# Six expert slots instead of four, with the residual parked in DRAM, in a hybrid attention, delta-rule and MoE layer

## The reference

```python
x = x + g1 * mix
h = rms_norm(x, norm2_w) * (1.0 + sc2) + sh2
x = x + g2 * hier_moe(h, ...)
...
def hier_moe(h, ...):               # 32 experts in 4 groups of 8
    grp = jnp.argmax(grp_logits, axis=-1)
    ...
    top_p, top_i = lax.top_k(jax.nn.softmax(in_grp, axis=-1), TOP_K)     # 2 of the group's 8
    wts = p_grp * top_p / jnp.sum(top_p, axis=-1, keepdims=True)
    ...
    hid = silu(h @ w_exp_gate[e]) * (h @ w_exp_up[e])       # 1024 -> 256, twice
    hid = hid * combine[..., None]
    return einsum('blef,efd->bld', hid, w_exp_down)         # 256 -> 1024
```

## Time and profile before

| what | us |
|---|---|
| median of three runs | 1172.69 |
| profiled execution, its own time | 1173.27 |
| its span in the profile | 1171.5 |
| PE busy in the span | 1029.5 (88%) |
| VectorE busy | 433.0 (37%) |
| ScalarE busy | 311.7 (27%) |
| POOL busy | 164.0 (14%) |
| weights of the 28 experts loaded after the routing | 88.1 MB |

### The profile page before, as it was taken

One profiled execution on the slowest core, in us unless ns is written; L12 is line 12 of the kernel. 1 busy time (PEld: TensorE's weight loads), 2 busy tenths in 40 slices (PEclk: granted clock), 3 DMA queues, 4 the chain that ended last, 5 costly groups with the idle time before them and its releaser, 6 DMA issues.

```text
span 1171.5 us, 14600 instructions
## 1 busy us (share of the span) xinstructions
PE 1029.5 (88%) x5595; PEld 562.0 (48%) x5595; DVE 433.0 (37%) x845; ACT 311.7 (27%) x619; POOL 164.0 (14%) x257
## 2 busy tenths in 40 slices
PE   4999999999998889989999999999919997797870
PEld 2444456666554679988544444444513332232220
DVE  1433036787775864645501200224460111100116
ACT  4122144566652434324310000111211111111111
POOL 0100020011000327770300000000110121101110
PEclk9999999999999999999999999999959999988995
DMA  9821152436110111300371110142535999999956
GB/s 387 346 90 46 70 183 88 190 116 216 73 72 16 42 39 41 98 8 1 109 284 72 72 72 10 63 166 85 216 103 192 396 401 422 422 424 423 423 226 269
DMA packets 43644, 204.20 MB, mean 174 GB/s; under 512 B 16736, under 2 KB 22320, under 8 KB 31536
## 3 DMA queue, kind: packets, MB, share of 16 engines
q1 hardware_dynamic: 32576, 171.92, 37.3%
q0 software_dynamic: 10416, 30.45, 7.3%
q10 hardware_dynamic: 576, 0.82, 0.2%
HBM read 191.79 MB, written 19.76 MB: 181 GB/s over the span
## 4 chain that ended last, share of the span: by engine, by line
PE 75%; DVE 11%; issue 5%; DMA 5%; ACT 2%; POOL 2%; SPq 0%; POOLq 0%; DVEq 0%; ACTq 0%
PE bank L1717 25%; PE bank L2311 11%; PE bank L1839 7%; PE bank L2332 5%; PE bank L2156 3%; PE bank L2154 3%; PE bank L1681 2%; PE bank L1998 2%; PE bank L1888 2%; DMA arena<-in_w_up 2%; PE bank L2299 1%; PE bank L2008 1%; PE bank L1732 1%; DMA arena<-in_w_blocks 1%; PE bank L1824 1%
## 5 line engine op out<-in xcount | busy, mean ns | idle before, releaser
L1717 PE MATMUL bank<-arena 128*128 128x512 f32 x672 | 292.6, 591 | 0.0
L1717 PEld LDWEIGHTS bank<-arena 128*128 128x128 f32 x672 | 125.4, 189 | 151.8 <-issue 151.8
L2311 PE MATMUL bank<-arena 128*32 128x512 f32 x1152 | 140.5, 642 | 32.1 <-issue 30.8
L1839 PE MATMUL bank<-arena 128*128 128x320 f32 x384 | 120.0, 454 | 0.0
L2311 PEld LDWEIGHTS bank<-arena 128*32 128x32 f32 x1152 | 42.4, 117 | 117.9 <-issue 117.9
L1839 PEld LDWEIGHTS bank<-arena 128*128 128x128 f32 x384 | 69.7, 192 | 35.7 <-issue 11.2
L1649 DVE TENSOR_TENSOR arena<-arena,bank 128x256 f32<-128x256 f32 x18 | 7.6, 421 | 174.6 <-ACT arena L1104 174.6
L1493 DVE TENSOR_TENSOR arena<-arena,bank 128x512 f32<-128x512 f32 x10 | 6.9, 688 | 168.1 <-PE bank L2156 168.1
L2332 PE MATMUL bank<-arena 128*32 128x512 f32 x576 | 65.8, 595 | 1.0 <-DVE arena L1642 1.0
L1026 ACT ACTIVATE arena<-bank 128x512 f32<-128x512 f32 x20 | 12.0, 598 | 145.7 <-PE bank L1717 145.7
L1104 ACT ACTIVATE arena<-bank 128x256 f32<-128x256 f32 x18 | 6.9, 385 | 164.2 <-PE bank L2311 164.2
(11 more groups left out here) (315 smaller groups left out, 1387.7 us busy)
## 6 DMA issues: line engine op xcount, KB each, us to landing
arena<-in_w_up SPq DMA_DIRECT2D x32, 2048.0 KB, 18.1
arena<-in_w_blocks SPq DMA_DIRECT2D x27, 2048.0 KB, 8.0
arena<-in_w_down SPq DMA_DIRECT2D x32, 1024.0 KB, 21.9
arena<-y_scratch SPq DMA_DIRECT2D x10, 512.0 KB, 7.3
arena<-in_bias POOLq DMA_DIRECT2D x3, 1536.0 KB, 10.7
arena<-mod_scratch POOLq DMA_DIRECT2D x8, 512.0 KB, 10.9
arena<-in_x SPq DMA_DIRECT2D x5, 512.0 KB, 7.0
gram_scratch<-arena SPq DMA_DIRECT2D x10, 256.0 KB, 2.5
```

What stands on the lines that cost most here:

```text
L1717: last = mm(bank, hT[:, k, tok0[i]:tok0[i] + P], w[:, k, :], start=(k == 0), stop=(k == KC - 1))
L1839: last = mm(banks[5 + half][:, 0:HTOK], w[:, k, :], hT[:, k, half * HTOK:(half + 1) * HTOK], start=(k == 0), stop=(k == KC - 1))
L2311: last = mm(banks[2 + e % 2][at, :], rowsT[e % 2][:, k, at], eup[expert % SLOTS_W][:, k, :], start=(k == 0), stop=(k == KC - 1))
```

## The change

The four slots become six, numbered 0 to 5; experts 0 to 5 are loaded before the routing. Experts 6 to 23 use slot e % 6, experts 24 to 31 slot e % 4. The list of rows keeps its 2304 places and 18 tiles: ten experts of 96 rows, twenty of 64, and two of 32. The last tile thus holds experts 29, 30 and 31.

The room for slot 4's up is taken from `gate2_bc` and the small tensors behind it, that for slot 5's up from the residual `x2` itself; the down weights of both stand in pieces (two of 0.5 MB, four of 0.25 MB) in places that are free then. So `x2` is written to DRAM (`x_scratch`) after the mixing part, and `gate2_bc` is no longer loaded early; both are loaded by SP (`residual_back`) behind the last expert load, and VectorE waits for them before its last steps. The router gets one operation more for the offsets and two for the capacities. The norm's unused square goes to a part of `merged`, and some semaphores are merged under one name.

```diff
-SLOTS_W = 4
-N_WIDE, WIDE, NARROW = 8, 96, 64
+SLOTS_W, DENSE_W = 6, 4
+N_BIG, N_SMALL = 4, 2
+WIDE, NARROW, SMALL = 96, 64, 32
 N_RANKED = N_EXPERTS - SLOTS_W
-SLOTS = N_WIDE * WIDE + (N_EXPERTS - N_WIDE) * NARROW
+ROWS_OF = [WIDE] * (SLOTS_W + N_BIG) + [NARROW] * (N_RANKED - N_BIG - N_SMALL) + [SMALL] * N_SMALL
+SLOTS = sum(ROWS_OF)
+SLOT_OF = [e % SLOTS_W if e < N_EXPERTS - 2 * DENSE_W else e % DENSE_W for e in range(N_EXPERTS)]
...
+        def before(e):
+
+            return max(q for q in range(e) if SLOT_OF[q] == SLOT_OF[e])
...
+            def residual_back():
+                for c in range(2):
+                    row = bass.AP(t["mod_scratch"].tensor, 3 * KC * 2 * P + c * P, [[0, P], [2 * P, KC], [1, P]])
+                    sp.dma_start(gate2_bc[:, c, :].rearrange("p (k n) -> p k n", k=KC), row).then_inc(S["y_out"], 16)
+                for i in range(T):
+                    sp.dma_start(x2[:, i, :], t["x_scratch"][i]).then_inc(S["y_out"], 16)
...
             sp.wait_ge(S["x2_ready"], NHALF * T)
+            for i in range(T):
+                sp.dma_start(t["x_scratch"][i], x2[:, i, :]).then_inc(S["y_out"], 16)
             up_in(3)
+            sp.wait_ge(S["logit_mm"], 3)
+            down_in(5)
+            sp.wait_ge(S["y_out"], 16 * T)
+            sp.wait_ge(S["h_ready"], 2 * T)
+            sp.wait_ge(S["ssq_ready"], T + 1)
+            up_in(5)
+            down_in(4)
...
                 for n in range(TILES):
                     for q in range(SLOTS_W, N_EXPERTS):
-                        if last_tile(q - SLOTS_W) == n:
+                        if last_tile(before(q)) == n:
                             sp.wait_ge(S["eup_mm"], n + 1)
                             ranked_up(q)
...
+                sp.wait_ge(S["down_mm"], max(last_tile(e) for e in range(N_EXPERTS) if SLOT_OF[e] >= DENSE_W) + 1)
+                residual_back()
...
-            step(v.tensor_scalar(lists[:, L_CAP + SLOTS_W:L_CAP + N_EXPERTS], rank, float(n_big), float(NARROW - WIDE), ALU.is_lt, ALU.mult))
+            ranked_cap = lists[:, L_CAP + SLOTS_W:L_CAP + N_EXPERTS]
+            step(v.tensor_scalar(ranked_cap, rank, float(N_BIG), None, ALU.is_lt))
+            step(v.scalar_tensor_tensor(ranked_cap, rank, float(N_RANKED - N_SMALL), ranked_cap, ALU.is_lt, ALU.add))
+            step(v.tensor_scalar(ranked_cap, ranked_cap, -1.0, float(NARROW - WIDE), ALU.add, ALU.mult))
```

More of the change, by code:

```diff
@@ L259, in build @@
         gate1_bc = cut(2, D)
+        gate2_at = top[0]
         gate2_bc = cut(2, D)
@@ L322, in build @@
         rows_out = [flat(hT)[:, (2 + n) * D:(3 + n) * D] for n in range(3)]
-        slot_f = flat(merged)[:, 4 * D:4 * D + 2 * TILES]
-        empty = flat(merged)[:, 4 * D + 2 * TILES:4 * D + 4 * TILES]
-        slots = flat(merged)[:, 4 * D + 4 * TILES:4 * D + 6 * TILES].bitcast(I32).rearrange("p (n e) -> p n e", n=2)
+        slot_f, empty, slots = (flat(sgb)[:, HALF + n * 2 * TILES:HALF + (n + 1) * 2 * TILES] for n in range(3))
+        slots = slots.bitcast(I32).rearrange("p (n e) -> p n e", n=2)
         acc = rows_in + [flat(sgb)]
@@ L381, in y_loaded @@
         def y_loaded(i):
[L383 to L385 removed]
+            return S[f"w_in{i}"], expert_loaded(max(e for e in range(N_EXPERTS) if SLOT_OF[e] == i)) + 32
         def tile_parts(n):
[L389 to L391 removed]
+            owner = [e for e, rows_of in enumerate(ROWS_OF) for _ in range(rows_of // 32)]
+            return [(slice(32 * a, 32 * a + 32), owner[4 * n + a]) for a in range(4)]
         def last_tile(q):
@@ L557, in _ @@
             sp.wait_ge(S["mT_mm"], 2 * T)
-            for e in range(SLOTS_W):
+            for e in range(DENSE_W):
                 down_in(e)
+            sp.wait_ge(S["sqsum"], T)
+            sp.wait_ge(S["ob_ready"], T)
+            up_in(4)
             sp.wait_ge(*read_by("out0"))
@@ L568, in _ @@
             with sp.If(is_dense > 0):
[L569 to L572, removed]
+                for e in range(DENSE_W, SLOTS_W):
+                    sp.wait_ge(S[f"w_in{e}"], 16)
+                    sp.wait_ge(S[f"w_down_in{e}"], 16 * len(down_parts(e)))
+                residual_back()
+                for e in range(DENSE_W, N_EXPERTS):
+                    sp.wait_ge(S["down_mm"], T * (e - DENSE_W + 1))
+                    up_in(e, DENSE_W)
+                    down_in(e, DENSE_W)
             with sp.Else():
@@ L710, in _ @@
             pool.wait_ge(S["modrow_io"], 16)
[L711 removed]
+            for kind, dst in enumerate((gate1_bc, shift_bc, scale_bc)):
                 for c in range(2):
@@ L1555, in _ @@
             ranked_off = lists[:, L_OFF + SLOTS_W:L_OFF + N_EXPERTS]
-            n_big = N_WIDE - SLOTS_W
-            step(v.tensor_scalar(ranked_off, rank, -float(n_big), 0.0, ALU.add, ALU.max))
+            step(v.tensor_scalar(ranked_off, rank, -float(N_BIG), 0.0, ALU.add, ALU.max))
+            step(v.scalar_tensor_tensor(ranked_off, rank, float(N_RANKED - 1), ranked_off, ALU.is_ge, ALU.add))
             step(v.tensor_scalar(ranked_off, ranked_off, float(NARROW - WIDE), float(SLOTS_W * WIDE), ALU.mult, ALU.add))
@@ L1583, in _ @@
             step(v.scalar_tensor_tensor(slot_f, table, -1.0, empty, ALU.add, ALU.add))
-            step(v.tensor_copy(slots, slot_f.rearrange("p (n e) -> p n e", n=2)), "slots_ready")
+            step(v.tensor_copy(slots, slot_f.rearrange("p (n e) -> p n e", n=2)), "chosen")
             barrier(dve, 3)
@@ L2310, in up @@
                         for at, expert in tile_parts(e):
-                            last = mm(banks[2 + e % 2][at, :], rowsT[e % 2][:, k, at], eup[expert % SLOTS_W][:, k, :], start=(k == 0), stop=(k == KC - 1))
+                            last = mm(banks[2 + e % 2][at, :], rowsT[e % 2][:, k, at], eup[SLOT_OF[expert]][:, k, :], start=(k == 0), stop=(k == KC - 1))
                     last.then_inc(S["eup_mm"], 1)
```

104 lines of the change are left out of this document (63 added, 41 removed).

## The result

| | before | after |
|---|---|---|
| median of 20 runs, us | 1172.72 | 1174.43 |
| lowest and highest | 1170.32, 1177.03 | 1172.36, 1180.29 |
| profiled execution, us | 1173.27 | 1178.19 |
| its span | 1171.5 | 1176.1 |

The ratio on record is 1.0021, with a 95% interval of 1.0012 to 1.0031 (the quotient of the two medians is 1.0015): slower by 0.2%, less than the 0.3% that was set as the border of "no change". The forecast was 1167.5. The interval excludes a gain, and an equal time only just. The profiled execution of after lies 3.8 us above the median of its kernel, so a single difference of 2 or 3 us between the two profiles is not evidence by itself.

A forecast was written before the change was run, and what follows sets the result against it. Expert loads were taken as bound by the DMA pipe (421 GB/s) and by slots coming free. PE's end -7.3 us and tail +1.5 gave -5.8 on 1173.27: 1167.5 us, range 1159 to 1177 (forecast's own 1163 to 1171).

The forecast's parts named there:

- Two experts off the stretch, tile 16 earlier: Load-bound experts: 7.34 MB (17.4 us) fewer loads ahead, less 1 us idle, start tile 16 16.4 us earlier, at 1091.6.
- Tile 17's start: Last tile: up 31, issued at 1101.2 after tile 16's up, lands and lets tile 17 start at 1110.
- issue bound: Up 31's landing if loaded alone: 7.3 us after its issue at 1101.2, so 1108.5.
- byte bound: Up 31's landing behind two ups and two downs (6.29 MB, 14.9 us of pipe) and up 28: 1112.
- From tile 17 to the last matmul: End of experts: up 7.1, tile 16's down 4.1, wait for down 31, last down 3.7; PE ends at 1131.2.
- The tail: After the last matmul: residual and gate2 reload (3.67 MB) mostly hidden, slowing the last scatter: +1.5 us, range 0 to +7.5.
- the second rival: At the end, the reload holds up the last scatter, 10.1 us for 2.64: +7.5 us, 1173.5, no change; chance 0.20.
- Ahead of the routing: Before the first up tile: three more VectorE operations +0.6 us, first gather overlapping the early loads +0.5 us.
- The h write: Last write of h before the router: 2 us of slack beside the early loads, costed at 0.
- The pieces of the down loads: Down loads for slots 4 and 5 in 2 or 4 pieces: 0.33 us of SP a piece, under its waiting: 0.
- four fifths of the forecast's 0.50: Share of the forecast's chance lying under 1169.2 us, the line for faster; counted as 0.43 in a total of 0.55.
- the right two waits: At the end, expert 31 takes expert 27's slot: up 31 waits for tile 16's up, down 31 for its down.

The follow-up runs named there:

- x2: Changed kernel without the reload of the residual and gate2 behind the last expert load, computing y on what lies there: 1171.69 us, ratio 0.9996.
- x3: Changed kernel with up 5, down 4 and down 5 issued behind the first gathers instead of ahead of the routing: 1173.59 us, ratio 1.0004.
- x5: Changed kernel with useless matmuls (19, 14 and 12) in TensorE's three last waits, which stood twice as long as the waits: 1184.56 us, ratio 1.0105.
- x6: Changed kernel with its own list of rows but six slots to the end (e % 6): 1172.48 us, ratio 1.0001.
- x8: Changed kernel with both the list of rows of x1 and the six slots to the end of x6: 1163.06 us, ratio 0.9917.
- x9: x5 with about half the useless matmuls (9, 7 and 6) in TensorE's three last waits: 1174.39 us, ratio 1.0016.
- x1: Changed kernel with eight experts of 96 rows and 24 of 64, so the last tile holds two experts, 30 and 31: 1164.67 us, ratio 0.9946.
- x10: x8 with up 5, down 4 and down 5 issued behind the first gathers, as in x3: 1164.42 us, ratio 0.9920.
- x4: Kernel before, four slots, with the changed kernel's list of rows alone (three experts in the last tile): 1186.27 us, ratio 1.0117.
- x7: x1 with the reload of the residual and gate2 moved ahead of the last four downs: 1169.15 us, ratio 0.9974.

## Why the prediction was wrong

The direction was wrong: 0.4% faster was forecast, 0.2% slower came. Step by step:

- **Two experts off the stretch, tile 16 earlier.** Forecast 1091.6, measured 1094.1. TensorE ran without a wait to tile 12 and had its first stall at tile 13 (4.59 us at 1034.5), as forecast. Right in kind; the 2.5 us were not traced to a cause (x2 has tile 16 at 1094.4 and x3 at 1092.8).
- **Tile 17's start: wrong by 5.3 us.** Forecast 1110, measured 1115.3. Up 31 was to leave at 1101.2 and left at 1104.60, since tile 16 started 2.5 us later and its up took 9.72 us for 8.8. It was to land 8.8 us after its issue and took 10.5. I had put it between an issue bound (1108.5) and a byte bound (1112). Worked out again from where tile 16 really started, the first gives 1104.6 + 7.3 = 1111.9 and the second 1094.1 - 2.3 + 14.9 + 5.0 + 2.3 = 1114.0. The byte bound comes nearer, and there was no reason to go below it, but both are too early; what held up 31 for the rest is not shown. In five other runs up 31 lands between 1113.1 and 1114.5 (x3, x5, x6, x8, x9), though it is issued anywhere from 1074.9 to 1106.4; in x1 and x10 it lands at 1109.6, so 1114 is no fixed floor.
- **From tile 17 to the last matmul: wrong by 2.8 us.** Forecast 21.2 us, measured 24.0 (15.7 before). Down 31 was forecast to land in 5.8 us (4.8 and the 1.0 added) and took 5.26; with its issue that wait is 5.8 us for 6.2. What was missing is the lower clock behind the waits: 9.35 for 7.1 us in the up, 4.94 for 3.7 in the down, 3.5 us that the sum held at nothing. I had used the row of 8.78 us for tile 16, since it stood behind a stall in the trace, and then let tile 17 and the last down, which stand behind stalls that the change makes, run at full speed. x5 shows the three pieces at full speed when TensorE is kept busy, and x9 shows that two of them back at full speed don't shorten the kernel.
- **The tail: wrong by 2.3 us.** Forecast +1.5, measured +3.8 (33.7 for 29.9); x2 prices the reload at 2.9 us by the ratios. The mechanism was named as the second rival, the last scatter beside the reload, with 7.5 us as its price; the truth lies between. It was not that the terms ahead had slipped, since the scatter slipped with them. The reload was to be landed 14.0 us after the issue of down 31; its last load landed 18.4 us after it (1128.80 to 1147.2), and SP was not done issuing it before 1136.1. So it stood beside the scatter to its end (1147.6) and not only with its tail.
- **Ahead of the routing.** +1.1 us forecast for the first up tile, +1.05 measured. The number was right in part by luck: from VectorE's wait for h on it is +2.1 us, and the execution came to that wait 1.05 us earlier. The router's steps cost 0.4 us for 0.6, the gather 1.4 for 0.5, and 0.3 lie between the gather and the up. The engines were not empty at 869.3: up 5 landed at 868.9, and down 4 stood behind it. The h write was in time, as forecast.
- **The pieces of the down loads.** Costed at 0.33 us each, that is at nothing. Single issues took up to 8.9 us, and a load that waited for tile 13's up (ended at 1049.01) left at 1055.56. The DMA share was 1.02 over 1040 to 1060, so the engines had work meanwhile; no run shows a cost in time, and none rules it out.

The sum of the misses, 2.5 + 2.8 (tile 17's other part) + 2.8 + 2.3, is 10.4, and the profiled execution of after is off the forecast by 10.7 (1178.19 for 1167.5). By the medians the miss is 6.9 us, since the profiled execution of after lies 3.8 us above its kernel's median.

The chances hold a slip of their own: four fifths of the forecast's 0.50 are 0.40 and not 0.43, so "faster" had 0.52.

The cause that decides the sign is the list of rows joined to the rule of slots. x4 shows that the new list on four slots costs 13.7 us, which is nearly the whole worth of two experts (14.9); in the changed kernel it costs 8.8 (x1). Undoing it alone turns the change into a gain of 0.5%, with six slots to the end as well into 0.8% (x8). The step of the prediction that failed is the price of this mechanism. It had the mechanism, with the right two waits, and priced the loss between tile 16's start and the last matmul at 8 us (15.3 of lead, 7.3 left); it was 13.6 (12.8 of lead, -0.8 left). The second term that was too small is the tail, 1.5 for 3.8.

What stays open: why up 31 took 10.5 us to land; whether the loads ahead of the routing cost 1 or 2 us or nothing in the kernel's time; and why x1, without the two waits, has its last matmul only 8.3 us earlier than the kernel before, where 14.9 us of pipe time left the stretch. The engines were a little less full there (share 0.97 over 980 to 1120, 1.01 before).

## What to carry to other kernels

When loads are taken off a stretch bound by DMA, the gain can end where the last load may first be issued: look at what the last tile waits for, and at the last one down to its issue, before counting megabytes. When two lower bounds of a start are at hand, one by issue and one by bytes, the estimate should not lie below the later one. A long wait that the change makes can also slow the matmuls behind it, as it did here; keeping TensorE busy through it gains nothing where the next load sets the end (x9).

## What the runs showed of the hardware

Behind its long waits TensorE ran at a lower granted clock. In the changed kernel the up tile behind 8.7 us of waiting has a PEclk of 0.72 and takes 9.72 us; with TensorE busy through most of the wait (x9) it has 1.00 and takes 7.09. That is the step between the two levels, 2.4 and 1.2 GHz, for part of the tile: an estimate from these rows is 5.4 us at the lower and 4.3 at the upper level, which does the work of 7.0 us at the upper one with a mean of 0.72.

The issue of a load can itself block SP. In the trace before a ranked down's issue takes at most 0.333 us and a ranked up's at most 0.645; in the changed kernel the longest take 8.9 and 5.8 us, and in x7 two loads in runs of 512 B held SP for 12.6 us, right behind two ups of 2 MB. Since the whole ups block too, the pieces alone don't explain it; six slots also let more loads stand outstanding, and no run separates the two. The line of the ranked downs before, and in the changed kernel:

```profile
L584 SPq DMA_DIRECT2D arena<-in_w_down x28: 332/333/333, 900.7 to 1121.0; - x28
```

```profile
L635 SPq DMA_DIRECT2D arena<-in_w_down x38: 332/333/8895, 902.4 to 1128.8; - x38
```
